# ScalarE's order of work in a hybrid attention block: the probability copy put ahead of the exponentials, eight weight high parts put ahead of a wait

## The chip, the cores and the metric

The kernel runs on one core of a Trainium2 chip, as one program written engine by engine: TensorE (PE) multiplies, ScalarE (ACT) and VectorE (DVE) work elementwise, GpSimd (POOL) does too, SyncE (SP) issues most transfers. The metric is the time of one execution in device microseconds. All times below are microseconds from the start of the profiled execution's span unless they are marked otherwise.

## What is computed

The reference is one layer on an input of 1024 tokens by 1024 features, in float32:

```python
h = rms_norm(x, g_mix[l])
p = h @ w_in[l]
aq, ak, av, mq, mk, mv, mo, mi, mf = jnp.split(p, split_idx, axis=-1)
...
att = sliding_window_attention(aq, ak, av, attn_sinks[l], slopes)
...
mix = jnp.concatenate([rms_norm(att, g_attn_out[l]), rms_norm(mh, g_mlstm_out[l])], axis=-1)
x = x + mix @ w_out[l]
h2 = rms_norm(x, g_ffn[l])
x = x + (jax.nn.silu(h2 @ w_gate[l]) * (h2 @ w_up[l])) @ w_down[l]
```

The attention has 8 query heads and 2 key-value heads of width 64, a window of two chunks of 64 keys, a distance penalty and a learned sink for each head. `mh` is the output of a chunkwise matrix-memory recurrence (mLSTM).

## The kernel before

The tokens are cut into T = 8 tiles of 128. Each large product is computed as three PE passes on split operands, high part times high part and the two cross terms (`three`, lines 878 to 880), so each weight block needs a high part (`w_hi`, a copy with rounding) and a low part (`w_lo`, the remainder). For the key-value weights, eight blocks of 128x264, ScalarE makes the high parts (`w_high(n)`, line 1410) and POOL the low ones (`split`, line 739), each waiting for its high part. The blocks of the later groups are 128x512.

The work between the first product and the feed-forward network is a loop over U from 8 to 55, written out for each engine (line 1106 for PE, 1481 for ACT, 1888 for DVE). U // 8 is the group of columns and U % 8 the tile. Units 8 to 15 make keys, values and gates, 16 to 31 the mLSTM inputs, 32 to 39 the queries, and 40 to 55 are the output projection (`out_unit`, two parts of 12 matmuls). Nothing reorders this: every engine takes its instructions in the written order, and each waits for counted semaphores.

At the start ScalarE sums the squares of the rows of x, computes the row scales (`row_scales`), and sends them through memory to every partition: `store_rows(b)` waits for a transpose by DVE (`rpadT`) and issues four stores, `load_rows(b)` waits for these and issues one load. DVE meanwhile runs the short convolution (lines 1820 and 1822). ScalarE later applies a table change and a SiLU to each convolution result (line 1491).

The attention of tile t takes several values of U. With s = U - 32:

- PE transposes the normalised queries of tile s - 1 (line 1010), ScalarE copies them out as `qT` (line 1544), and PE computes the scores of tile s - 2 (line 1027) after them.
- DVE adds the penalty (line 2086), finds the row maxima `nmx` (lines 2096 and 2097), and ScalarE takes eight exponentials in place in `prob` (line 1582) and one of the sinks (`esk`, line 1585), for tile s - 2.
- In the next U, DVE inverts the sums (lines 1851 and 1852) and normalises one half of `prob` (line 1855); POOL normalises the other half (`normalise`, line 762), and then splits one block of the output weights (lines 735, 737 and 739).
- In the middle of the unit after that, PE transposes the eight blocks of `prob` of tile s - 4 (`att_prob_transposes`, line 1040). ScalarE copies the first half to `pT` (line 1536), DVE the second (line 1846). At the unit's end PE multiplies them with the values (`att_values`, line 1065). This product also waits for `qT` of tile s - 1.
- DVE scales the raw queries to `qn` (line 2107), after the row maxima of the same U. Units 38 and later wait for `qn` because it empties their accumulator bank; the second part of unit 40 waits for `qn` of tile 7.

Of the kernel before, what the change touches and what calls it, by code (L numbers as in the profile page):

```python
# [30 lines left out]
ACT = mybir.ActivationFunctionType  # L31
# [43 lines left out]
def hymba_block(nc, x, g_mix, w_in, b_gates, conv_qk, q_gain, k_gain, sinks,  # L75
# [3 lines left out]
    T = S // P  # L79
    K = D // P  # L80
# [29 lines left out]
    with ctx:  # L110
# [13 lines left out]
        def sem(name):  # L124
            return ctx.enter_context(nc.semaphore(name))
# [116 lines left out]
        qT, prob, pT = [qT0, qT1], [prob0, prob1], [pT0, pT1]  # L242
# [40 lines left out]
        bank = [banks[i // 2][:, i % 2, :] for i in range(8)]  # L283
# [94 lines left out]
        pt_done = sem("p_transposed")  # L378
        pTa = sem("pT_act")
        pTd = sem("pT_dve")  # L380
        pv_done = sem("pv_done")
# [55 lines left out]
        def raw_count(n):  # L437

            return sum(16 * len(slice_source(m)) for m in range(K + n % RAW, n + 1, RAW))
# [870 lines left out]
        def _(act):  # L1310
            steps = [0]

            def step(ins):
                steps[0] += 1
                ins.then_inc(act_step, 1)

            def link(ins):

                step(ins)
                act.wait_ge(act_step, steps[0])  # L1320

            def inverse_root(out_, sumsq, n):

                link(nc.scalar.activation(out_, sumsq, ACT.Ln, bias=eps_t[0:sumsq.shape[0], 0:1], scale=1.0 / n))
                return nc.scalar.activation(out_, out_, ACT.Exp, scale=-0.5)
# [10 lines left out]
            def row_scales(b):  # L1336

                act.wait_ge(x_sq, 4 * b + 4)
                tt = slice(4 * b, 4 * b + 4)
                inverse_root(rstd[:, tt], stat[:, tt], D).then_inc(rstd_ready, 1)  # L1340

            def store_rows(b):

                act.wait_ge(rstd_turned, b + 1)
                if b == 1:
                    act.wait_ge(rstd_s, 16)
                rows = rstd_dram[b:b + 1, :].rearrange("a (t q j) -> q (a t) j", q=4, j=32)
                for q in range(4):
                    act.dma_start(rows[q], rpadT[32 * q:32 * q + 4, b, :]).then_inc(rows_stored, 16)

            def load_rows(b):
                act.wait_ge(rows_stored, 16 * 4 * (b + 1))
                act.dma_start(rstd_b[:, b * H:(b + 1) * H],
                              rstd_dram[b:b + 1, :].to_broadcast([P, H])).then_inc(rstd_s, 16)
# [45 lines left out]
            def w_high(n):  # L1400

                g, k = 1 + n // K, n % K
                width = NKV if g == 1 else N
                if g == 1:
                    act.wait_ge(w1_s, 16 * 2)
                    w = w1_raw[:, k, :]
                else:
                    act.wait_ge(raw_s[n % RAW], raw_count(n))
                    w = w_raw[:, n % RAW, 0:width]
                nc.scalar.activation(w_hi[:, (g * K + k) % RING, 0:width], w, ACT.Copy).then_inc(w_act_hi, 1)  # L1410
# [17 lines left out]
            for t in range(4, T):  # L1428
                square_sum(t)
            row_scales(1)  # L1430
            for n in range(4):
                w_high(n)
            store_rows(1)
            for n in range(4, K):
                w_high(n)
            load_rows(1)
            act.wait_ge(mq_done, 2)
            w_high(K)
# [42 lines left out]
            for U in range(T, ALL):  # L1481
# [33 lines left out]
                s = U - 3 * T  # L1515
# [12 lines left out]
                if 1 <= s < T:  # L1528
                    state_squares(s - 1)
                s = U - 4 * T  # L1530
                if 0 <= s - 4 < T:
                    tt = s - 4
                    act.wait_ge(pt_done, tt + 1)
                    if tt >= 2:
                        act.wait_ge(pv_done, tt - 1)
                    nc.scalar.activation(pT[tt % 2][:, 0:4, :], bank[6][:, :].rearrange("p (k n) -> p k n", k=4),
                                         ACT.Copy).then_inc(pTa, 1)
                if 0 <= s - 1 < T:
                    tt = s - 1

# [9 lines left out]
                if 0 <= s - 1 < T:  # L1550
                    tt = s - 1
# [10 lines left out]
                if 0 <= s - 4 < T:  # L1562
                    tt = s - 4
# [7 lines left out]
                if 0 <= s - 6 < T:  # L1571
                    tt = s - 6
                    act.wait_ge(ssa_ready, tt + 1)
                    inverse_root(rmix[:, tt, :], ss2[:, tt, :], N).then_inc(rmix_ready, 1)
                if 0 <= s - 2 < T:
                    tt = s - 2
                    act.wait_ge(s_max, tt + 1)
                    if tt >= 1:
                        act.wait_ge(p_ready[0], tt)
                        act.wait_ge(p_ready[1], tt)  # L1580
                    for j in range(8):
                        step(nc.scalar.activation(prob[tt % 2][:, j, :], prob[tt % 2][:, j, :], ACT.Exp, bias=nmx[:, j:j + 1],  # L1582
                                                  accum_out=dsum[:, j:j + 1]))
                    act.wait_ge(sink_shift, tt + 1)
                    nc.scalar.activation(esk[:, :], esk[:, :], ACT.Exp).then_inc(p_exp, 1)
                s = U - 6 * T
# [713 lines left out]
```

## Time and profile before

| | us |
|---|---|
| median of 3 runs | 992.14 |
| lowest and highest run | 991.68, 992.31 |
| the profiled execution | 992.37 |
| its span | 990.6 |
| PE, busy | 983.1 |
| DVE, ACT, POOL, busy | 652.9, 422.9, 667.2 |

The span is the stretch in which engines work; the rest of the profiled execution's time lies around it. PE's clock is granted in full throughout. A row of the timeline gives the start, the duration, the engine, the line, the operation, what is written and read, the shape, how many instructions are merged, and in brackets how long the engine stood idle before and what released it. Matmul durations overlap: the next one starts before the one before has ended, so the distance between starts is what one costs.

### The profile page before, as it was taken

How to read it: one execution, taken by the hardware profiler on the slowest of the kernel's cores; microseconds unless marked ns; L12 is line 12 of the kernel's file. 1: busy time of each engine (PE TensorE's matmuls, PEld its weight loads, DVE VectorE, ACT ScalarE, POOL GpSimd, SP SyncE). 2: the span in 40 equal slices, each digit the busy share in tenths (PEclk: the TensorE clock that was granted, in tenths of full speed). 3: DMA queues.
4: the chain of work that ended last, by engine and by line, in shares of the span. 5: the costliest groups of instructions: out<-in, count | busy, mean ns of one | idle time of the engine just before them, and what ended most of it. 6: DMA issues, size and time to landing. Idle time of an engine off the chain costs nothing.

```text
span 990.6 us, 13176 instructions
## 1 busy us (share of the span) xinstructions
PE 983.1 (99%) x4816; PEld 814.8 (82%) x4816; DVE 652.9 (66%) x808; ACT 422.9 (43%) x868; POOL 667.2 (67%) x529
## 2 busy tenths in 40 slices
PE   9999999999999999999999999999999999999998
PEld 7898888878888888888888888888888888888887
DVE  5596345569843696958757485866748577674485
ACT  5542155467622665525243342524334352433440
POOL 0164466626784328978868777877877787887792
PEclk9999999999999999999999999999999999999999
DMA  8634435541321002121121121122112112112213
GB/s 294 211 85 81 110 79 138 138 164 33 108 65 32 22 22 85 54 64 43 43 86 44 43 73 55 43 60 68 43 43 85 43 43 80 48 42 62 78 58 134
DMA packets 103592, 76.87 MB, mean 78 GB/s; under 512 B 30696, under 2 KB 83944, under 8 KB 103528
## 3 DMA queue, kind: packets, MB, share of 16 engines
q1 hardware_dynamic: 102168, 75.00, 25.2%
q10 hardware_dynamic: 1360, 1.02, 0.4%
q8 instruction: 39, 0.64, 0.3%
q14 instruction: 25, 0.20, 0.1%
HBM read 68.15 MB, written 7.36 MB: 76 GB/s over the span
## 4 chain that ended last, share of the span: by engine, by line
PE 90%; DVE 3%; DMA 2%; ACT 1%; SPq 1%; issue 1%; POOL 0%; ACTq 0%; DVEq 0%
PE banks L878 29%; PE banks L880 28%; PE banks L879 28%; DMA x_in<-in_x 1%; PE banks L1065 1%; PE banks L891 1%; PE banks L968 1%; ACT prob L1582 1%; PE banks L1040 1%; PE banks L980 0%; DMA rstd_b<-rstd_rows 0%; PE banks L1027 0%; DMA rstd_rows<-rpadT 0%; PE banks L990 0%; PE banks L953 0%
## 5 line engine op out<-in xcount | busy, mean ns | idle before, releaser
L808 POOL TENSOR_TENSOR wr_lo<-wr_raw,wr_hi 128x512 fp32r<-128x512 f32 x231 | 319.0, 1412 | 27.1 <-ACT wr_hi L1394 21.9
L802 POOL TENSOR_TENSOR wr_raw<-wr_raw,wr_raw 128x512 f32<-128x512 f32 x132 | 193.6, 1471 | 132.3 <-PE banks L880 72.7
L878 PE MATMUL banks<-hf_hi,wr_hi 128*128 128x512 f32 x616 | 240.2, 390 | 0.0
L879 PE MATMUL banks<-hf_lo,wr_hi 128*128 128x512 f32 x616 | 239.8, 389 | 0.0
L880 PE MATMUL banks<-hf_hi,wr_lo 128*128 128x512 f32 x616 | 239.8, 389 | 0.0
L1394 ACT ACTIVATE wr_hi<-wr_raw 128x512 fp32r<-128x512 f32 x231 | 136.6, 625 | 165.0 <-POOL wr_raw L802 106.0
L2246 DVE TENSOR_TENSOR x<-banks,x 128x1024 f32<-128x1024 f32 x138 | 168.8, 1225 | 51.5 <-PE banks L880 35.2
L878 PE MATMUL banks<-w_hi,actT_hi 128*128 128x512 f32 (+1 forms) x384 | 147.1, 383 | 0.9 <-POOL w_lo L739 0.8
L880 PE MATMUL banks<-w_hi,actT_lo 128*128 128x512 f32 (+1 forms) x384 | 143.3, 373 | 0.0
L879 PE MATMUL banks<-w_lo,actT_hi 128*128 128x512 f32 (+1 forms) x384 | 143.0, 372 | 0.0
L878 PEld LDWEIGHTS banks<-hf_hi,wr_hi 128*128 128x128 f32 x616 | 115.7, 188 | 24.4 <-issue 0.4
L880 PEld LDWEIGHTS banks<-hf_hi,wr_lo 128*128 128x128 f32 x616 | 115.7, 188 | 24.0
L879 PEld LDWEIGHTS banks<-hf_lo,wr_hi 128*128 128x128 f32 x616 | 115.7, 188 | 23.8
L878 PE MATMUL banks<-wr_hi,af_hi 128*128 128x512 f32 x308 | 120.0, 390 | 0.2 <-DVE x L2246 0.2
L879 PE MATMUL banks<-wr_lo,af_hi 128*128 128x512 f32 x308 | 119.9, 389 | 0.0
L880 PE MATMUL banks<-wr_hi,af_lo 128*128 128x512 f32 x300 | 116.8, 389 | 0.0
L2140 DVE TENSOR_TENSOR af_raw<-banks,af_raw 128x512 f32<-128x512 f32 x33 | 22.8, 691 | 128.9 <-PE banks L880 128.9
L739 POOL TENSOR_TENSOR w_lo<-w_raw,w_hi 128x512 fp32r<-128x512 f32 (+1 forms) x48 | 62.0, 1298 | 56.0 <-ACT w_hi L1410 53.4
L2164 DVE TENSOR_TENSOR af_lo<-af_raw,af_hi 128x512 fp32r<-128x512 f32 x75 | 88.8, 1226 | 0.3
L878 PEld LDWEIGHTS banks<-w_hi,actT_hi 128*128 128x128 f32 x384 | 72.2, 188 | 14.8 <-issue 1.4
L880 PEld LDWEIGHTS banks<-w_hi,actT_lo 128*128 128x128 f32 x384 | 72.2, 188 | 12.9
L879 PEld LDWEIGHTS banks<-w_lo,actT_hi 128*128 128x128 f32 x384 | 72.3, 188 | 11.4
(206 smaller groups left out, 1201.5 us busy)
## 6 DMA issues: line engine op xcount, KB each, us to landing
wr_raw<-in_w_up SPq DMA_DIRECT2D x46, 256.0 KB, 3.2
wr_raw<-in_w_gate SPq DMA_DIRECT2D x44, 256.0 KB, 3.4
wr_raw<-in_w_down SPq DMA_DIRECT2D x44, 256.0 KB, 3.1
w_raw<-in_w_in SPq DMA_DIRECT2D x32, 256.0 KB, 3.6
x_in<-in_x SPq DMA_DIRECT2D x4, 1024.0 KB, 13.1
w_raw<-in_w_out SPq DMA_DIRECT2D x16, 256.0 KB, 2.7
x<-in_x SPq DMA_DIRECT2D x8, 512.0 KB, 6.1
out<-x SPq DMA_DIRECT2D x16, 256.0 KB, 2.1
```

The lines of the kernel that those rows point to most:

```text
L739: nc.gpsimd.tensor_tensor(w_lo[:, ring, 0:width], w, w_hi[:, ring, 0:width].bitcast(F32), ALU.subtract).then_inc(w_ready, 1)
L802: nc.gpsimd.tensor_tensor(wr_raw[slot(q, f)][:, :], wr_raw[slot(q, a)][:, :], wr_raw[slot(q, b)][:, :], ALU.subtract).then_inc(wsum, 1)
L808: nc.gpsimd.tensor_tensor(wr_lo[s][:, :], wr_raw[s][:, :], wr_hi[s][:, :].bitcast(F32), ALU.subtract).then_inc(wf_lo, 1)
L878: nc.tensor.matmul(ps, x_hi, wh, start=first, stop=False, skip_group_check=more)
L879: nc.tensor.matmul(ps, x_hi, wl, start=False, stop=False, skip_group_check=more)
L880: return nc.tensor.matmul(ps, x_lo, wh, start=False, stop=last, skip_group_check=more)
L891: last = nc.tensor.transpose(bank[2 + b][:, j * P:(j + 1) * P], h2buf[t % 2][:, (4 * b + j) * P:(4 * b + j + 1) * P], ident[:, :])
L968: last = nc.tensor.matmul(bank[6 + i][:, value_region(pair)], scd[:, 2 * pair + i, :], mvx[:, t, 2 * pair + i, :], start=pair == 0, stop=t ...
L1394: nc.scalar.activation(wr_hi[s][:, :], wr_raw[s][:, :], ACT.Copy).then_inc(wf_hi, 1)
L2140: V_.tensor_tensor(dst[:, :], src[:, :], dst[:, :], ALU.add).then_inc(added, 1)
L2164: V_.tensor_tensor(af_lo[b][f][:, :], af_raw[b][f][:, :], af_hi[b][f][:, :].bitcast(F32), ALU.subtract).then_inc(act_lo_s, 1)
L2246: V_.tensor_tensor(xs, banks[first + h][:, :, :], xs, ALU.add).then_inc(down_add, 1)
```

## The change

There are two moves of ScalarE instructions, and no instruction is added or taken away. At the start, `w_high(4)` to `w_high(7)` stand ahead of `store_rows(1)`, where before they stood behind it. In the attention, the copy of the transposed probabilities to `pT` stood at the head of the body for tile s - 4, ahead of the query copy. Now it stands one U earlier, for tile s - 3, directly ahead of the exponentials of tile s - 2.

```diff
             row_scales(1)
-            for n in range(4):
+            for n in range(K):
                 w_high(n)
             store_rows(1)
-            for n in range(4, K):
-                w_high(n)
             load_rows(1)
             act.wait_ge(mq_done, 2)
             w_high(K)
...
                 s = U - 4 * T
-                if 0 <= s - 4 < T:
-                    tt = s - 4
-                    act.wait_ge(pt_done, tt + 1)
-                    if tt >= 2:
-                        act.wait_ge(pv_done, tt - 1)
-                    nc.scalar.activation(pT[tt % 2][:, 0:4, :], bank[6][:, :].rearrange("p (k n) -> p k n", k=4),
-                                         ACT.Copy).then_inc(pTa, 1)
                 if 0 <= s - 1 < T:
...
                     inverse_root(rmix[:, tt, :], ss2[:, tt, :], N).then_inc(rmix_ready, 1)
+                if 0 <= s - 3 < T:
+                    tt = s - 3
+                    act.wait_ge(pt_done, tt + 1)
+                    if tt >= 2:
+                        act.wait_ge(pv_done, tt - 1)
+                    nc.scalar.activation(pT[tt % 2][:, 0:4, :], bank[6][:, :].rearrange("p (k n) -> p k n", k=4),
+                                         ACT.Copy).then_inc(pTa, 1)
                 if 0 <= s - 2 < T:
                     tt = s - 2
                     act.wait_ge(s_max, tt + 1)
```

ScalarE at the start, before. The rows L1410 with 128x264 are the high parts of the key-value weights, L1349 the stores of the row scales, L1353 their load:

```order
L1324 ACTIVATE rstd<-stat,cols 128x4
L1325 ACTIVATE rstd<-rstd 128x4
L1410 ACTIVATE w_hi<-w_raw 128x264 x4
L1349 DMA rstd_rows<-rpadT 4x32 x4
L1410 ACTIVATE w_hi<-w_raw 128x264 x4
L1353 DMA rstd_b<-rstd_rows 128x512
L1410 ACTIVATE w_hi<-w_raw 128x512
L1447 ACTIVATE kvs<-banks,rstd 128x264
```

The same place after the change, where L1445 is the first evacuation of a key-value unit:

```order
L1324 ACTIVATE rstd<-stat,cols 128x4
L1325 ACTIVATE rstd<-rstd 128x4
L1410 ACTIVATE w_hi<-w_raw 128x264 x8
L1349 DMA rstd_rows<-rpadT 4x32 x4
L1353 DMA rstd_b<-rstd_rows 128x512
L1410 ACTIVATE w_hi<-w_raw 128x512
L1445 ACTIVATE kvs<-banks,rstd 128x264
```

The last four high parts have moved from behind the stores, and their wait, to ahead of them; the load follows the stores directly.

ScalarE in the attention, from the end of U = 36 into U = 38, before. The rows L1582 are the exponentials, L1536 is the copy to `pT`, L1544 that to `qT`:

```order
L1567 ACTIVATE sqb<-banks 128x512
L1568 ACTIVATE actT_hi<-banks 128x4x128
L1582 ACTIVATE prob_137,dsum<-prob_137,nmx 128x128 x8
L1585 ACTIVATE esk<-esk 128x8
L1536 ACTIVATE pT_143<-banks 128x512
L1544 ACTIVATE qT_135<-banks,cols 128x512
L1470 ACTIVATE pq<-banks,rstd 128x512
L1554 ACTIVATE actT_hi<-mh 128x4x128
```

The same place after the change, where L1580 are the exponentials, L1571 is the copy to `pT` and L1535 that to `qT`:

```order
L1558 ACTIVATE sqb<-banks 128x512
L1559 ACTIVATE actT_hi<-banks 128x4x128
L1571 ACTIVATE pT_143<-banks 128x512
L1580 ACTIVATE prob_137,dsum<-prob_137,nmx 128x128 x8
L1583 ACTIVATE esk<-esk 128x8
L1535 ACTIVATE qT_135<-banks,cols 128x512
L1468 ACTIVATE pq<-banks,rstd 128x512
L1545 ACTIVATE actT_hi<-mh 128x4x128
```

The copy to `pT`, with its wait for PE's transposes of that tile, has moved from behind the eight exponentials and `esk` to ahead of them; the copy to `qT` now follows `esk` directly.

## Rows read from the trace of the kernel before

**Rows 1.** Page, first part: busy time of an engine, share, instructions

```profile
PE 983.1 (99%) x4816; PEld 814.8 (82%) x4816; DVE 652.9 (66%) x808; ACT 422.9 (43%) x868; POOL 667.2 (67%) x529
```

**Rows 2.** Waits of PE: us in total, times, longest

```profile
PE banks L1065 <- ACT qT L1544: 1.6, 1, 1.6
...
PE banks L878 <- POOL w_lo L739: 0.8, 2, 0.5
```

**Rows 3.** Timeline of PE, the first key-value unit (U = 8)

```profile
49.76 0.28 PE L878 MATMUL banks<-w_hi,actT_hi 128*128 128x264 f32 x1
...
50.12 0.29 PE L878 MATMUL banks<-w_hi,actT_hi 128*128 128x264 f32 x1
...
54.11 0.28 PE L878 MATMUL banks<-w_hi,actT_hi 128*128 128x264 f32 x1
```

**Rows 4.** Timeline of ACT, then of POOL, 42 to 57 us

```profile
49.12 1.05 ACT L1410 ACTIVATE w_hi<-w_raw 128x264 fp32r<-128x264 f32 x3 [5.71 <-issue]
...
42.55 3.54 POOL L739 TENSOR_TENSOR w_lo<-w_raw,w_hi 128x264 fp32r<-128x264 f32 x4 [40.76 <-ACT w_hi L1410]
49.62 7.36 POOL L739 TENSOR_TENSOR w_lo<-w_raw,w_hi 128x264 fp32r<-128x264 f32 x6 [3.53 <-ACT w_hi L1410]
```

**Rows 5.** Timeline of DVE and PE around the gates (U = 18)

```profile
89.55 0.19 DVE L1918 SCALAR_TENSOR_TENSOR lf<-gate,expf 128x32 f32<-128x32 f32 x1 [4.49 <-ACT expf L1507]
...
90.87 0.30 PE L1114 MATMUL banks<-lf,tri 128*128 128x32 f32 x2
```

**Rows 6.** Timeline of PE in the attention, transposes (L1040) and value products (L1065)

```profile
221.53 0.66 PE L1065 MATMUL banks<-pT,v_prev 128*64 128x128 f32 x8 [1.64 <-ACT qT L1544]
...
225.42 1.03 PE L1040 MATMUL banks<-ident,prob 128*128 128x128 f32 x8
...
230.66 0.66 PE L1065 MATMUL banks<-pT,v_prev 128*64 128x128 f32 x8
...
234.78 1.03 PE L1040 MATMUL banks<-ident,prob 128*128 128x128 f32 x8
```

**Rows 7.** Timeline of ACT in the attention, 217 to 230 us

```profile
217.04 0.40 ACT L1582 ACTIVATE prob<-prob,nmx 128x128 f32<-128x128 f32 x1 [3.17 <-DVE nmx L2097]
...
220.24 0.57 ACT L1536 ACTIVATE pT<-banks 128x512 f32<-128x512 f32 x1
220.71 0.67 ACT L1544 ACTIVATE qT<-banks,cols 128x512 f32<-128x512 f32 x1
...
225.93 0.40 ACT L1582 ACTIVATE prob<-prob,nmx 128x128 f32<-128x128 f32 x1 [1.71 <-DVE nmx L2097]
...
229.68 0.69 ACT L1544 ACTIVATE qT<-banks,cols 128x512 f32<-128x512 f32 x1
```

**Rows 8.** Timeline of DVE, then of POOL, 229 to 236 us

```profile
234.15 0.65 DVE L2097 TENSOR_TENSOR nmx<-nmx,nsink 128x8 f32<-128x8 f32 x1
...
235.66 0.69 DVE L2107 TENSOR_TENSOR qn<-banks,qscale 128x512 f32<-128x512 f32 x1
...
229.74 1.54 POOL L762 TENSOR_TENSOR prob<-prob,dsum 128x512 f32<-128x512 f32 x1 [2.64 <-DVE dsum L1852]
...
233.48 1.29 POOL L739 TENSOR_TENSOR w_lo<-w_raw,w_hi 128x512 fp32r<-128x512 f32 x1
```

**Rows 9.** Timeline of DVE and PE in unit 40: last `qn`, second part

```profile
253.91 0.69 DVE L2107 TENSOR_TENSOR qn<-banks,qscale 128x512 f32<-128x512 f32 x1
...
254.65 0.50 PE L878 MATMUL banks<-w_hi,actT_hi 128*128 128x512 f32 x1
```

**Rows 10.** Timeline of DVE, POOL and PE around unit 42

```profile
273.28 0.68 DVE L1846 COPY pT<-banks 128x512 f32<-128x512 f32 x1
...
270.09 1.29 POOL L739 TENSOR_TENSOR w_lo<-w_raw,w_hi 128x512 fp32r<-128x512 f32 x1
...
263.26 1.03 PE L1040 MATMUL banks<-ident,prob 128*128 128x128 f32 x8
...
275.87 0.66 PE L1065 MATMUL banks<-pT,v_prev 128*64 128x128 f32 x8
```

## The prediction

> **What bounds the kernel now.** I read the busy times first. PE works 983.1 of the 990.6 us of the span [rows 1], so all of its idle time is 7.5 us, and the two moves touch no PE instruction. The second view is the list of PE's waits, which says where ScalarE's order costs PE anything: 1.6 us in one place, a value product waiting for the copy of queries `qT`, and 0.8 us in two places, the first key-value unit waiting for low weight parts [rows 2]. The timelines around these two places give the rest. In both, the thing to see is the distance between starts on PE with nothing late, and how early each of its inputs was. Everything behind them is a long stretch in which PE waits for nothing, so a microsecond won or lost there should reach the end unchanged.
>
> **First edit, the high parts.** Unit 8 on PE takes its triples of matmuls 0.36 us apart while nothing is late (49.76, 50.12), so its eight triples need 2.88 and unit 9 would start at 52.64. It starts at 54.11 [rows 3]. The late inputs are the low parts of blocks 4 to 7: POOL stood idle 3.53 us for their high parts, and ScalarE made these from 49.12 on, after 5.71 us without work behind the wait for the row scales [rows 4]. With the change ScalarE makes them in that idle stretch, from about 43.4, at 0.35 each (1.05 for three), done at 44.8. POOL made the first four low parts in 3.54, 0.885 each, to 46.09, and goes straight on with the other four, to 49.6. Block 4 is wanted at 51.2. PE waits for none of them: **54.11 - 52.64 = 1.47 us gained**.
>
> What hides the moved work is ScalarE's idle stretch of 5.71 us, of which 1.4 are used. The stores, which come behind, were waiting for DVE and leave as before. What the earlier POOL work may cost is DVE's time: it now runs beside the turning of the row scales, before 49.12. If DVE were held for one low part at each of two small instructions, the stores would leave 1.8 later, near 51, and the load and the next high part would follow; unit 8 ends at 52.64 and only then does ScalarE have to evacuate it. So I take nothing, with 0 and 1.8 us on a covered path as the ends.
>
> Does the gain live on? PE's next close meeting is at unit 18, where the gate sums were ready at 89.74 and wanted at 90.87 [rows 5]. They came out of ScalarE (`expf`), which had been started by the evacuation of unit 17, that is by PE. So they move with PE and the slack of 1.1 stays. What does not move with PE is DVE's convolution before it; were it the last input, at most 1.47 - 1.13 = 0.34 would be lost. From there to unit 32 I let the whole stage move by 1.47.
>
> **Second edit, unit 36.** All times in this part are on the clock of the trace before. ScalarE's exponentials of tile 1 start at 217.04 and the next thing, then the `pT` copy, at 220.24, so a set with its sink takes 3.20; the copy delays what follows by 0.47 (220.24 to 220.71); and PE goes on 0.82 after `qT` starts (220.71 to 221.53) [rows 6, 7]. The transposes of tile 0 lie 5.24 ahead of the natural place of the value product (225.42 to 230.66), so near 214.7, done before 216. The `pT` copy therefore runs in an idle moment before 217.04 (3.17 idle there), and `qT` starts at 220.24: **0.47 us gained**, the value product at 221.06. It is not the whole 1.6, because the exponentials themselves are late.
>
> **Second edit, units 37 to 39.** Here the moved wait bites. Call P the moment when the eight transposes of a tile are done (start plus 1.03). Before, the exponentials of tile 2 started at 225.93, while P of tile 1 was 225.42 + 1.03 = 226.45 [rows 6, 7]. Now the exponentials stand behind the copy, which stands behind P. With 0.04 for a signal (DVE's row ended at 234.80 when POOL's ended at 234.77 [rows 8]), they start at P + 0.04 + 0.47 = P + 0.51, and `qT` after them lets PE go on at P + 0.51 + 3.20 + 0.82 = P + 4.53. PE arrives there by itself at P + 4.21 (230.66 - 226.45). So PE loses 0.32 us in each unit. That the margin is this thin shows already in the trace: `qT` started at 229.68, would have let PE go at 230.50, and PE came at 230.66 [rows 6, 7].
>
> Is P really the later of the two inputs in every unit? The maxima are held by POOL. From exponentials to POOL's normalisation it is 3.81 (225.93 to 229.74), and from there to the end of its low part 5.03 (234.77), when the row maxima end too [rows 8]. So maxima are ready 8.9 us after the last exponentials started. PE's period is 9.36 (225.42 to 234.78) plus the new 0.32, so P wins in each: **3 x 0.32 = 0.96 us lost** (units 37, 38, 39). The sum of the edit is now -0.47 + 0.96 = +0.49.
>
> **Second edit, unit 40.** The second part of this unit waits for the last `qn`, which ended at 254.60, and PE went on at 254.65 [rows 9]. `qn` starts 0.89 after the end of POOL's low part (234.77 to 235.66) [rows 8]. On the new clock P of tile 3 is 226.45 + 2 x 9.36 = 245.17 plus the shift at that time, -0.47 + 2 x 0.32 = 0.17, so 245.34. The exponentials of tile 4 start at 245.85, POOL at 249.66, its low part ends at 254.69, `qn` starts at 255.58 and ends at 256.27, and PE goes on at 256.32. That is 1.67 after 254.65, so the shift jumps **from 0.49 to 1.67**.
>
> **Second edit, unit 42.** P of tile 5 is 263.26 + 1.03 + 1.67 = 265.96, the exponentials of tile 6 start at 266.47, POOL ends its low part 8.84 later at 275.31. DVE's own `pT` copy started 1.90 after that point (273.28 against 270.09 + 1.29) and takes 0.68, so it ends at 277.89, and PE wants it at 275.87 + 1.67 = 277.54 [rows 10]. With 0.05 for the signal PE loses 0.4, and the edit stands at **+2.1**. Behind it the exponentials are over and nothing else hangs on ScalarE's order.
>
> **Sum.** -1.47 + 2.1 = +0.6 us. The profiled execution has 992.37, so it would have 993.0; the median of the runs is 0.23 below it, at 992.14, which gives **992.8 us**. A measurement of this kernel tells about 0.2% (2 us) from no change.
>
> **A rule beside a row.** The row maxima on DVE (line 2097, a tiny instruction) took 0.65 us and ended within 0.03 of POOL's low part [rows 8]. The Trainium skill, page "SBUF — State Buffer", section "Who interferes with whom", says that a DVE instruction with two inputs in SBUF is blocked while a GpSimd instruction that reads SBUF runs; by that rule, the trace agrees. It speaks against the first edit, since POOL's four low parts come to lie over DVE's work of 46 to 49.6 us; the third rival is what it would make of the time.
>
> **Rivals.**
> - The stalls of the attention are smaller than worked out. Each of the 0.32 rests on sums of starts; if PE arrives later or the copy costs less, only the jumps go. With no stall at units 37 to 42, the result is -1.47 - 0.47 = -1.9 us, 990.2. For it: PE's margin was positive before. Against it: exponentials behind P is plain order, and `qn` hangs on the same chain. Chance 0.07.
> - The stalls at 37 to 39 come and those behind them don't, since DVE is freer than I think: -1.47 + 0.49 = -1.0, 991.2. Chance 0.15.
> - Slower: the gain at the start is lost before unit 32, because DVE, held by POOL from 46 us on, ends the convolutions later and the gates with them, and the attention's loss stays. It gives 992.14 + 2.1 = 994.2, the edge of what can be told; it decides if DVE is over 1.1 us later at unit 18. If in addition the stall of 0.32 repeats in units 40 and 41, it is 994.9. For it: DVE was busy without a break there. Against: the contention is moved rather than added. Chance 0.13.
> - The copy's move does nothing at all, because PE's transposes are early: only the start counts, 990.7. P at 226.45 against 225.93 speaks against it. Chance 0.03.
>
> **Numbers.** My forecast has 0.62. Its cases and the second rival end within 2 us. Slower by over 0.2% (above 994.1) is most of the third rival: 0.11. Faster by over 0.2% (below 990.2) is half of the first and some unseen gain: 0.06. The rest, 0.83, is no change. The range goes from 991.0, which takes in the second rival, to 994.3, which takes in the third's first form.
>
> **What would show it.** In the profile after: unit 9 starts on PE near 52.6; POOL's eight small low parts follow each other; the wait of PE for low parts is gone. In the attention each set of exponentials starts directly behind a `pT` copy, half a microsecond after PE's transposes, and PE's wait for `qT` is spread over four units, about 1.2 in the first and 0.3 in the others. PE waits some 1.5 us in unit 40 for `qn` and some 0.4 in unit 42 for DVE's `pT`. I am wrong if units 37 to 39 keep 9.36 between transposes, or if the units before 32 are not about 1.5 us earlier.

## The result and the profile after

| | median | lowest to highest | profiled execution | its span |
|---|---|---|---|---|
| before | 992.12 us | 991.32 to 993.19 (16 runs) | 992.37 us | 990.6 us |
| after | 993.78 us | 993.12 to 995.01 (16 runs) | 993.57 us | 991.8 us |

The ratio is 1.0019, with a 95% interval from 1.0012 to 1.0026: the change costs 1.66 us in the medians and 1.2 us between the two profiled executions. The forecast was a cost of 0.6 us. The time lies in the range and counts as no change by the forecast's bound of 0.2%, but its interval is wholly on the slow side and reaches past that bound, so the result is a small loss rather than nothing.

The first part of the page, to stand against [rows 1], and the list of PE's waits, to stand against [rows 2] (us in total, times, longest), both of the kernel after:

```profile
PE 983.3 (99%) x4816; PEld 814.7 (82%) x4816; DVE 657.4 (66%) x808; ACT 422.5 (43%) x868; POOL 667.3 (67%) x529
...
PE banks L1065 <- ACT qT L1535: 1.9, 3, 1.2
PE banks L878 <- DVE qn L2105: 1.2, 1, 1.2
...
PE banks L1065 <- issue: 0.4, 1, 0.4
```

PE does the same work in the same time. The wait for low parts is gone, and the one wait for `qT` has become three. Two waits are new: one for `qn`, and one of a value product in unit 42, which the list puts down to no releaser ("issue"). DVE's copy to `pT` is the last input there, ended at 277.00 with the product at 277.11 (DVE, after):

```profile
276.33 0.67 DVE L1844 COPY pT<-banks 128x512 f32<-128x512 f32 x1
```

The kinds of waits are those that the prediction said would be seen. One of its signs of being wrong did come: it asked for the units before 32 to be about 1.5 us earlier, and they are 1.0 earlier, as follows.

The start, PE's timeline after (start, length, engine, line, operation), against [rows 3] and [rows 5]:

```profile
50.52 0.28 PE L878 MATMUL banks<-w_hi,actT_hi 128*128 128x264 f32 x1
...
53.40 0.28 PE L878 MATMUL banks<-w_hi,actT_hi 128*128 128x264 f32 x1
...
89.88 0.30 PE L1114 MATMUL banks<-lf,tri 128*128 128x32 f32 x2
```

Unit 8 takes exactly the 2.88 us worked out, with no wait. It starts at 50.52 and not at 49.76, so unit 9 starts only 0.71 earlier than before (53.40 against 54.11), and the gates of unit 18 are 0.99 earlier (89.88 against 90.87). At the first query transposes, where the attention begins, the lead is 1.03 (195.85 against 196.88).

The attention, PE's timeline after, to stand against [rows 6, 9, 10]:

```profile
195.85 0.60 PE L1010 MATMUL banks<-ident,qn 128*128 128x128 f32 x4
...
220.00 0.66 PE L1065 MATMUL banks<-pT,v_prev 128*64 128x128 f32 x8 [1.16 <-ACT qT L1535]
...
223.89 1.03 PE L1040 MATMUL banks<-ident,prob 128*128 128x128 f32 x8
...
229.56 0.66 PE L1065 MATMUL banks<-pT,v_prev 128*64 128x128 f32 x8
...
239.33 0.66 PE L1065 MATMUL banks<-pT,v_prev 128*64 128x128 f32 x8 [0.37 <-ACT qT L1535]
...
253.21 1.03 PE L1040 MATMUL banks<-ident,prob 128*128 128x128 f32 x8
...
255.45 0.50 PE L878 MATMUL banks<-w_hi,actT_hi 128*128 128x512 f32 x1 [1.21 <-DVE qn L2105]
...
277.11 0.66 PE L1065 MATMUL banks<-pT,v_prev 128*64 128x128 f32 x8 [0.37 <-issue]
...
291.78 0.28 PE L1000 MATMUL banks<-ones,sqb 128*128 128x1 f32 x2
```

Read it as a distance from the first row, since everything before it only moves the clock. From 195.85 to the last product of squares, at the end of unit 44, it is 95.93 us. Before it was 93.65, from the first to the last of these rows of PE (before; the one between is the transposes of unit 40):

```profile
196.88 0.63 PE L1010 MATMUL banks<-ident,qn 128*128 128x128 f32 x4
...
253.50 1.03 PE L1040 MATMUL banks<-ident,prob 128*128 128x128 f32 x8
...
290.53 0.28 PE L1000 MATMUL banks<-ones,sqb 128*128 128x1 f32 x2
```

**The second edit costs 2.28 us** in this pair of executions, in four steps: PE gains 0.50 in unit 36, and loses 0.41 in each of units 37 to 39, 1.09 in unit 40 and 0.44 in unit 42. The stall in unit 37 has no bracket in its row, but shows in the distances: the value product comes 5.67 after its transposes (229.56 - 223.89), where it was 5.24. The transposes from 223.89 to 253.21 are three periods of 9.77; before they were 9.36.

Why ScalarE is late stands in its own timeline after, against [rows 7]:

```profile
224.96 0.60 ACT L1571 ACTIVATE pT<-banks 128x512 f32<-128x512 f32 x1 [2.25 <-PE banks L1040]
225.45 0.39 ACT L1580 ACTIVATE prob<-prob,nmx 128x128 f32<-128x128 f32 x1
...
228.63 0.67 ACT L1535 ACTIVATE qT<-banks,cols 128x512 f32<-128x512 f32 x1
```

The copy waits 2.25 us for the transposes, which end at 223.89 + 1.03 = 224.92. The eight exponentials follow it directly, 0.53 us after that end (P + 0.53 in the prediction's terms), and `qT` after them. The row maxima of this tile were there at 224.86 (next block), before the copy was done: the exponentials start 0.59 us after them, behind the copy. DVE, then POOL, after, against [rows 8]:

```profile
223.64 1.22 DVE L2095 TENSOR_TENSOR nmx<-nmx,nsink 128x8 f32<-128x8 f32 x1
...
223.55 1.28 POOL L739 TENSOR_TENSOR w_lo<-w_raw,w_hi 128x512 fp32r<-128x512 f32 x1
```

The tiny minimum with the sink ends with POOL's low part again, within 0.03 us, and now lasts 1.22 for a work that took 0.65 before. It starts sooner relative to POOL, so the hold shows longer.

### The profile page after: what moved, and what is told of

Same layout as the page of the kernel before. It is cut to its first block, busy times and chain, and to the rows that moved or that the text cites. A ratio compares the mean times of both kernels' runs of the same rounds, so it can differ in the third digit from the quotient of the medians.

```text
span 991.8 us, 13176 instructions
## 1 busy us (share of the span) xinstructions
PE 983.3 (99%) x4816; PEld 814.7 (82%) x4816; DVE 657.4 (66%) x808; ACT 422.5 (43%) x868; POOL 667.3 (67%) x529
## 4 chain that ended last, share of the span: by engine, by line
PE 94%; DVE 3%; ACT 2%; issue 1%; DMA 0%; SPq 0%; ACTq 0%; DVEq 0%
PE banks L878 28%; PE banks L880 28%; PE banks L879 28%; PE banks L933 2%; PE banks L937 1%; PE banks L942 1%; ACT prob L1580 1%; PE banks L1065 1%; PE banks L891 1%; PE banks L968 1%; PE banks L1040 1%; PE banks L980 0%; PE banks L990 0%; PE banks L953 0%; DVE prob L2084 0%
## 5 line engine op out<-in xcount | busy, mean ns | idle before, releaser
L2244 DVE TENSOR_TENSOR x<-banks,x 128x1024 f32<-128x1024 f32 x138 | 168.8, 1224 | 51.5 <-PE banks L880 35.2
```

The source lines that it names most:

```text
L2244: V_.tensor_tensor(xs, banks[first + h][:, :, :], xs, ALU.add).then_inc(down_add, 1)
```

## The experiments

Two theories stood against each other on the start: the edit gives back PE's whole wait in unit 8 (1.47), or part of it is lost again or was never there. On the attention: the copy's wait ahead of the exponentials makes the stalls, or late row maxima do. All the kernels of this section ran on one chip, in two groups of runs, each group with its own runs of the kernel before (992.24 us in the first, 992.12 in the second). A stage distance below is always that of PE from the first query transposes to the last product of squares, as above.

**The kernel before again**, run like a changed one, to see how far two executions of one program differ.

> The kernel before, unchanged, for its profile on the same chip: both theories expect the same time as before and, at the start, a scatter of unit 8's first matmul that does not come from the edits; theory A expects it to be as large as the 0.8 us by which unit 8 started later in the profile of the change.

Measured: 992.13 us (991.82 to 992.44), ratio 1.0000 [0.9992, 1.0009]. Its stage distance is 93.62 us, against 93.65: one program repeats this distance within 0.03 us here, from two executions. Its start is not so steady. PE's timeline, unit 8's first matmul, a wait inside unit 8, and unit 9:

```profile
50.53 0.28 PE L878 MATMUL banks<-w_hi,actT_hi 128*128 128x264 f32 x1
...
53.39 0.39 PE L878 MATMUL banks<-w_hi,actT_hi 128*128 128x264 f32 x1 [0.18 <-POOL w_lo L739]
...
53.87 0.28 PE L878 MATMUL banks<-w_hi,actT_hi 128*128 128x264 f32 x1
```

The same program starts unit 8 at 50.53 where the trace of before has 49.76 [rows 3], and yet reaches unit 9 at 53.87 and not at 54.11. Here the wait for low parts is worth some 0.5 us, not 1.47.

**The first edit alone.**

```diff
-            for n in range(4):
+            for n in range(K):
                 w_high(n)
             store_rows(1)
-            for n in range(4, K):
-                w_high(n)
             load_rows(1)
```

> Only the first edit: all eight high parts ahead of the wait for the row scales. Theory A (the start edit gains, the attention edit loses): unit 9 starts 2.88 us after unit 8 where it was 4.35 before, the whole later stage is 1.5 us earlier, and the median is 1.2 to 1.5 us below before (ratio 0.9985 to 0.9988). Rival B (the start edit gives nothing, because something else in the first 90 us takes its place): the median is within 0.4 us of before, and unit 18 is reached at the same time as before.

Measured: 991.25 us (990.43 to 992.37), ratio 0.9992 [0.9983, 1.0001]: 1.0 us below before, with an interval that just takes in no change. Its stage distance is 93.60, unchanged, as it must be. In the profiled execution unit 8 starts late, at 51.01, because PE had waited for the weights of the very first product:

```profile
9.71 1.17 PE L933 MATMUL banks<-actT_hi,w_hi 128*128 128x512 f32 x4 [1.06 <-ACT w_hi L1398]
...
51.01 0.28 PE L878 MATMUL banks<-w_hi,actT_hi 128*128 128x264 f32 x1
...
53.89 0.28 PE L878 MATMUL banks<-w_hi,actT_hi 128*128 128x264 f32 x1
```

Unit 9 is then reached at 53.89, no sooner than in the kernel before run again (53.87). So the edit does what it says, with unit 8 at 2.88 us, and is worth as much as the start of unit 8 allows.

**The second edit alone.**

```diff
-                if 0 <= s - 4 < T:
-                    tt = s - 4
...
-                    nc.scalar.activation(pT[tt % 2][:, 0:4, :], bank[6][:, :].rearrange("p (k n) -> p k n", k=4),
-                                         ACT.Copy).then_inc(pTa, 1)
...
+                if 0 <= s - 3 < T:
+                    tt = s - 3
...
+                    nc.scalar.activation(pT[tt % 2][:, 0:4, :], bank[6][:, :].rearrange("p (k n) -> p k n", k=4),
+                                         ACT.Copy).then_inc(pTa, 1)
                 if 0 <= s - 2 < T:
                     tt = s - 2
```

> Only the second edit: every copy of transposed probabilities ahead of the next exponentials. Theory A: the median is 2.1 to 2.5 us above before (ratio 1.0021 to 1.0025), made of -0.5 in unit 36, +0.4 in each of units 37 to 39, +1.1 in unit 40 and +0.4 in unit 42. Rival B: it makes the whole loss of the change by itself, 1.2 to 1.7 us, and the start edit adds nothing.

Measured: 994.30 us (994.01 to 994.70), ratio 1.0023 [1.0014, 1.0031]: 2.06 us above before. Its stage distance is 96.27 us, which is 2.6 above the 93.65. That is 0.3 more than in the kernel after. 0.16 of it is the stall of tile 2 (0.53 where that has 0.37). Most of the rest lies in unit 36, which gains 0.37 and not 0.50: the value product comes 24.28 us after the first query transposes, against 24.65 before and 24.15 after, since the maxima and with them the exponentials are 0.12 us later in this distance. It has the same waits as the kernel after; PE's list:

```profile
PE banks L1065 <- ACT qT L1537: 2.1, 3, 1.2
PE banks L878 <- DVE qn L2107: 1.2, 1, 1.2
...
PE banks L1065 <- issue: 0.4, 1, 0.4
```

The loss is the copy's own and needs nothing of the first edit.

**The copy moved for tiles 0 to 2 only**, the others left in their old place: if each moved copy costs by itself, the loss ends where the moved copies end.

```diff
-                if 0 <= s - 4 < T:
+                if 0 <= s - 4 < T and s - 4 >= 3:
...
+                if 0 <= s - 3 < T and s - 3 < 3:
```

> The second edit for tiles 0 to 2 only; the copies of tiles 3 to 7 stay behind the exponentials; no start edit. Theory A (exponentials wait behind the copy; the last scaled queries and DVE's copy hang on the same chain): the exponentials of tile 4 start with the row maxima again, 0.8 us earlier than with all copies moved, so the wait in unit 40 shrinks from 1.2 to about 0.8 and the one in unit 42 is gone: 0.9 us above before (0.6 to 1.3). Rival C (the waits in units 40 and 42 come from something else than the late copies): still 1.8 or more above before.

Measured: 993.18 us (992.62 to 993.72), ratio 1.0010 [1.0001, 1.0019]: 0.94 above before. The stage distance is 94.61, 0.96 above before, so time and distance agree. PE's timeline, value products of tiles 2 and 3, and unit 40:

```profile
240.52 0.66 PE L1065 MATMUL banks<-pT,v_prev 128*64 128x128 f32 x8 [0.37 <-ACT qT L1544]
...
249.91 0.66 PE L1065 MATMUL banks<-pT,v_prev 128*64 128x128 f32 x8
...
255.78 0.50 PE L878 MATMUL banks<-w_hi,actT_hi 128*128 128x512 f32 x1 [0.75 <-DVE qn L2114]
```

The stall is there for the last moved copy and gone for the first that was not moved. The wait for `qn` in unit 40 is shorter by 0.46, about the one stall that is missing, and the wait in unit 42 is gone, as was expected. This is the picture of the copy ahead of the exponentials, once per moved copy, and a `qn` that carries the delay on. It speaks against a cause that would act on all tiles alike.

**First edit, and the copy of tile 0 alone moved.** It asks how much of the gain of unit 36 stays.

```diff
-                if 0 <= s - 4 < T:
+                if 0 <= s - 4 < T and s - 4 >= 1:
...
+                if 0 <= s - 3 < T and s - 3 < 1:
```

> The first edit, and the second for tile 0 only. Theory A: unit 36 gains 0.5 us, but unit 37 then waits for the query copy, whose margin was 0.16, so it gives 0.3 back: together 1.6 us below before, 0.15 below the first edit alone. Rival D (what unit 36 gains stays): 1.9 to 2.0 us below before, 0.5 below the first edit alone.

Measured: 990.99 us (990.23 to 992.26), ratio 0.9989 [0.9980, 0.9998]: 1.25 below before, where 1.6 was expected, and 0.26 below the first edit alone, which is within the noise. The stage distance is 93.65, that of the kernel before: the gain of 0.50 in unit 36 was given back whole. PE's timeline:

```profile
224.41 1.03 PE L1040 MATMUL banks<-ident,prob 128*128 128x128 f32 x8
...
230.01 0.66 PE L1065 MATMUL banks<-pT,v_prev 128*64 128x128 f32 x8
```

The value product of unit 37 comes 5.60 after its transposes, not 5.24. With PE 0.5 us earlier and the exponentials where they were, the next `qT` is the late one by 0.36, of which 0.3 was expected; most of the rest goes in a wait of 0.2 for `qn` in unit 40, which was not. The step that I had left out is that a gain on PE shortens the slack of every later input too, if that did not move with it.

This kernel also shows the third rival in small. Its row scales for the convolution came late, and ScalarE's SiLU with it; ACT, then PE:

```profile
69.57 1.06 ACT L1489 ACTIVATE qkT<-qkT 128x1024 f32<-128x1024 f32 x1 [2.23 <-DVE qkT L1827]
70.54 0.46 ACT L1445 ACTIVATE kvs<-banks,rstd 128x264 f32<-128x264 f32 x1
...
71.05 0.39 PE L878 MATMUL banks<-w_hi,actT_hi 128*128 128x264 f32 x1 [0.29 <-ACT kvs L1445]
```

An evacuation of PE's banks stood behind a SiLU that waited for DVE, and PE waited 0.29 for it. From unit 9 to unit 18 this execution takes 37.09 us; the kernel after and the first edit alone take 36.48. Most of DVE's delay was there before the moved high parts ran: its scaling of the rows ahead of the convolution began at 42.43, against 41.02 in the kernel after, and the first high part started at 43.54. So the moved work did not start it; what did was not tried by itself.

**First edit, and the sink as a column of the scores.** The maxima are what unit 36 waits for. Here each block of scores gets a column that holds the sink, and one reduction over 129 columns takes the place of a reduction and a minimum; the other uses of `prob` read the first 128 columns, so the kernel computes the same.

```diff
-        prob0, e = place("prob0", [P, 8, P], at=e)
+        prob0, e = place("prob0", [P, 8, P + 1], at=e)
...
+                        if kv == 0 and tt < 2:
+                            V_.tensor_copy(prob[tt][:, :, P], sink_b[:, :])
...
-                    link(V_.tensor_reduce(nmx[:, :], prob[tt % 2][:, :, :], AX.X, ALU.max, negate=True))
-                    V_.tensor_tensor(nmx[:, :], nmx[:, :], nsink[:, :], ALU.min).then_inc(s_max, 1)
+                    V_.tensor_reduce(nmx[:, :], prob[tt % 2][:, :, :], AX.X, ALU.max,
+                                     negate=True).then_inc(s_max, 1)
```

> The first edit, copies where they stood before, and the row maxima without their second instruction: the sinks stand as a 129th column of each block of prob, so that one reduction gives the maximum over scores and sink and no tiny DVE instruction waits for the end of POOL's low part. Theory E (POOL holds that tiny instruction, and through it the exponentials, so the maxima are 0.2 to 1.3 us late in each tile): exponentials of tile 1 start 1.2 us earlier, PE's wait in unit 36 falls from 1.6 to 0.4, no wait comes up in unit 37, the 0.36 in unit 40 goes too: 1.3 to 1.7 us below the first edit alone, 2.3 to 2.7 below before. Rival F (the next small instructions are held in its place and the time of the exponentials does not change): the same as the first edit alone, 1.0 below before.

Measured: 989.40 us (988.80 to 991.12), ratio 0.9977 [0.9968, 0.9986]: 2.7 below before, the first kernel here whose gain is large beside the noise. The stage distance is 92.10, 1.50 shorter than with the first edit alone, and this is what the column gives by itself: 1.13 of it in unit 36 (the transposes of tile 4 lie 55.45 after the first query transposes and not 56.58), 0.37 in unit 40. DVE, POOL and ACT of this kernel:

```profile
212.80 1.23 DVE L2097 TENSOR_REDUCE nmx<-prob 128x8 f32<-128x1032 f32 x1
214.06 1.00 DVE L2100 TENSOR_TENSOR esk<-sink_b,nmx 128x8 f32<-128x8 f32 x1
...
213.74 1.29 POOL L739 TENSOR_TENSOR w_lo<-w_raw,w_hi 128x512 fp32r<-128x512 f32 x1
...
214.06 0.40 ACT L1580 ACTIVATE prob<-prob,nmx 128x128 f32<-128x128 f32 x1 [2.13 <-DVE nmx L2097]
```

The reduction runs through while POOL is at work and ends at 214.03, a microsecond before POOL (215.03), and the exponentials start at once. The instruction that is now held to POOL's end is `esk` (214.06 + 1.00 = 215.06), for which nobody waits here. The Trainium skill, page "SBUF — State Buffer", section "Who interferes with whom", says that an instruction of DVE with two SBUF inputs contends with a GpSimd instruction that reads SBUF, and that `tensor_reduce` on trn2 never does. The trace agrees with both: 1.23 us for the reduction under POOL, and an end within 0.03 of POOL's for `esk`.

**The same, with the copy of tile 0 moved**, by the condition of the kernel with the first edit and that copy.

> As e5, with the copy of tile 0 ahead of the exponentials of tile 1. Theory E: the rest of the wait in unit 36 goes as well: 0.3 to 0.4 below e5, 2.7 to 3.1 below before. Rival F: as the first edit with copy 0 alone, 1.2 below before.

Measured: 989.56 us (988.79 to 990.99), ratio 0.9977 [0.9968, 0.9986]: equal to the kernel just above, where 0.3 to 0.4 less was expected. The stage distance is 91.91, 0.19 shorter, so there is a gain, but a small one, and the scatter of the start is larger than it. PE's wait for `qT` fell from 0.55 to 0.26, and a third to a half of that went in the next unit, as in the kernel without the column.

**Both edits and the sink column**: the kernel after with the diff above. If late maxima made the stalls of units 37 to 39, this kernel loses them. If the copy's wait makes them, they stay.

> Both edits as in the change, and the sink column of e5. With all copies ahead of the exponentials these wait for PE's transposes, not for the maxima. Theory A with E: units 37 to 39 still lose 0.3 to 0.4 each, since earlier maxima don't help, and the chain behind the late exponentials stays: 1.5 to 2.5 us above e6, and 0.5 to 1.5 below before. Rival F (the exponentials were late because of the maxima, not because of the copy's wait): the three stalls go and it equals e6.

Measured: 993.06 us (991.54 to 993.50), ratio 1.0005 [0.9996, 1.0014]. It was expected below before, and is 0.9 above. Against the kernel just above it was expected 1.5 to 2.5 us slower: the medians differ by 3.5, the stage distances by 2.45 (94.36 against 91.91). DVE, ACT and PE:

```profile
222.38 1.23 DVE L2097 TENSOR_REDUCE nmx<-prob 128x8 f32<-128x1032 f32 x1
...
224.95 0.60 ACT L1571 ACTIVATE pT<-banks 128x512 f32<-128x512 f32 x1 [2.26 <-PE banks L1040]
225.45 0.39 ACT L1580 ACTIVATE prob<-prob,nmx 128x128 f32<-128x128 f32 x1
...
239.36 0.66 PE L1065 MATMUL banks<-pT,v_prev 128*64 128x128 f32 x8 [0.36 <-ACT qT L1535]
...
255.32 0.50 PE L878 MATMUL banks<-w_hi,actT_hi 128*128 128x512 f32 x1 [1.08 <-DVE qn L2108]
```

The maxima are there at 223.61, 1.84 us before the exponentials start, and the stalls stay: the transposes of tiles 1 to 4 are 9.80, 9.76 and 9.76 us apart, where the kernel with the column and no copy moved has 9.36 to 9.39. **So the copy's wait, and not the maxima, makes the stalls of units 37 to 39**: this is the run that decides it. In unit 42 it is otherwise. There PE no longer waits in this kernel (transposes of tile 5 to value product of tile 6: 12.63 us, against 12.61 before and 13.05 after), so that loss needed the second instruction of the maxima on DVE as well as the moved copy. The miss in the total fits a late start: unit 8 began at 51.52 in the profiled execution, unit 9 at 54.40, so the first edit gave nothing at all in it. That the median of the eleven runs has the same cause is not shown.

## Why the prediction was right, and where it was off

**The first edit: the mechanism was right, the size was one execution's.** "Its eight triples need 2.88" held in every kernel with the edit (50.52 to 53.40, 51.01 to 53.89). "So unit 9 would start at 52.64" did not: it takes the start of unit 8 at 49.76 as given. It is not. The ten profiled executions have 49.76, 50.53, 49.74 and 51.72 without the first edit, and 50.52, 51.01, 50.44, 49.77, 50.44 and 51.52 with it (two of them, 50.44, of different kernels), so the scatter is there without the edit too, and even between two executions of one program (49.76, 50.53). Without the edit, POOL's low parts hide a late unit 8: unit 9 starts at 54.11, 53.87, 53.81 and 54.60. With it, the same lateness reaches unit 9, at 53.40, 53.89, 53.32, 52.66, 53.32 and 54.40. The gain is 1.15 to 1.45 where unit 8 is at 49.77 (52.66 against 53.81 and 54.11), about 0.5 where it is at 50.5 (53.40 against 53.87), and nothing at 51.7. The mis-sized term is thus the 1.47, which measured 1.0 in the medians of the first edit alone. The spread of the runs points the same way: 0.6, 0.7 and 1.1 us from lowest to highest in the three kernels without the edit that had eleven runs each, 1.9 to 2.3 in those with it. It is not proof: the kernel before spread over 1.3 and 1.4 us in its 32 and 33 runs there, and over 1.9 in its 16 runs beside the kernel after. The kernel with first edit and sink column shows it best, with eight runs from 988.80 to 989.78 and three from 990.86 to 991.12.

**The cover of the moved work held.** I had taken nothing for it, with 1.8 us on a covered path as the other end. ACT after:

```profile
42.22 2.61 ACT L1410 ACTIVATE w_hi<-w_raw 128x264 fp32r<-128x264 f32 x8
48.89 1.29 ACTq L1349 DMA_DIRECT2D rstd_rows<-rpadT  x4
```

The stores leave at 48.89, 1.1 us later than before, and not "as before": DVE's small copy for them lasted 0.72 us beside POOL's low parts, against 0.16 before, and began 0.55 later, 0.38 of it from the three convolution instructions ahead of it (3.47 us, against 3.09). PE waited for none of it, as forecast.

**Unit 36** was sized at -0.47 and measured -0.50. **Units 37 to 39** were sized at 0.32 each and measured 0.41. The order of events was right, and the two spans in it were each a little longer: the exponentials start at P + 0.53, not P + 0.51, and from them to PE's going on it is 4.11 us (225.45 to 229.56), where I had added 3.20 and 0.82. So PE goes on at P + 4.64 instead of P + 4.53, against its own P + 4.21. **Unit 40**: the jump was put at +1.18 and is +1.09. The level that it reaches is 1.83 and not 1.67, because of the stalls ahead of it. I had not seen that the kernel before already waited here: its second part began 1.15 after its transposes [rows 9], and only 0.79 when `qn` is early, as with the sink column. **Unit 42**: put at +0.4, measured 0.44. The sum of the edit, 2.1 forecast, is 2.28 in the profile and 2.06 in the run of the second edit alone.

**The sum.** The rise was forecast at 0.6 us and measured 1.66 in the medians: direction and mechanism were right, the size was not, and the time is in the range because the range was wide (991.0 to 994.3). In the profiled execution I forecast 993.0 and it is 993.57. Of the 0.57 that is missing, 0.44 is the start (a lead of 1.03 and not 1.47 at the first query transposes) and 0.2 the attention. The medians of the two edits alone, -1.0 and +2.06, add up to 1.07; the change measured 1.66. The 0.6 between them is within what the intervals allow (each is 0.9 us to either side) and I don't explain it further. Sixteen runs after fall in two groups again, nine from 993.12 to 993.79 and seven from 994.35 to 995.01, and their median is the upper edge of the first.

**The rivals.** Smaller stalls, or none behind unit 39: refuted, by the kernel after and by the second edit alone. The copy does nothing: refuted, since it costs 2.06. The start gain lost through a late DVE: not in the kernel after, whose stretch from unit 9 to 18 is as short as any (36.48); 0.6 us were lost in that way in one other kernel, whose DVE was late for the most part before the moved work began. So the time came nearer to this rival's 994.2 than to the forecast's 992.8, but by another way: the start's own scatter and larger stalls.

## What to carry to other kernels

An instruction moved ahead of others on an engine brings its wait along, and everything behind it then starts after that wait: compare when its input arrives with when theirs do, in the steady loop and not only in the one unit where the gain is seen. A wait read from one execution is an offer only as large as the arrival at it is steady; run the unchanged kernel once more and see whether the place moves before putting its whole length in a sum. And when the late input is a tiny two-input VectorE instruction beside GpSimd, take the instruction away rather than reorder its users: this gave 1.5 us here in the stage distance (2.7 in the medians together with the first edit), where moving the copies cost 2.1 to 2.3.

## What the runs showed of the hardware

The first product's matmuls run at half pace in some executions. The first group of four matmuls after, in the kernel with the copies of tiles 0 to 2 (where the second group is slow too), and in the first edit with the sink column:

```profile
5.62 2.01 PE L933 MATMUL banks<-actT_hi,w_hi 128*128 128x512 f32 x4 [0.22 <-ACT w_hi L1398]
```

```profile
5.64 2.04 PE L933 MATMUL banks<-actT_hi,w_hi 128*128 128x512 f32 x4 [0.24 <-ACT w_hi L1398]
7.49 1.91 PE L937 MATMUL banks<-actT_lo,w_hi 128*128 128x512 f32 x4
```

```profile
5.74 1.16 PE L933 MATMUL banks<-actT_hi,w_hi 128*128 128x512 f32 x4 [0.63 <-ACT w_hi L1398]
```

The group takes 1.15 to 1.17 us in four executions and 1.84 to 2.05 in five, and each slow group puts unit 8 some 0.7 to 1.1 later: about 49.76 with none, 50.4 to 50.5 with one, 51.5 and 51.7 with two. The two executions that don't fit this had no group so slow (1.15 and 1.44) but late weights, a wait of 1.06 us for `w_hi` with the first edit alone (its row is above) and one of 0.59 with the copy of tile 0 moved:

```profile
17.31 1.16 PE L933 MATMUL banks<-actT_hi,w_hi 128*128 128x512 f32 x4 [0.59 <-ACT w_hi L1398]
```

The rows of the granted clock do not tell the slow stretch from the others (the first stretch of the kernel with the copies of tiles 0 to 2, which is slow, and then of the first edit with the sink column, which is not; columns: window, length, PE busy with its matmuls, granted clock, DMA share, GB/s):

```profile
5.50:7.40 1.90, 1.76 (x4) 1.00 0.98 308
```

```profile
5.50:7.40 1.90, 1.66 (x7) 1.00 0.90 264
```

Both give 1.00, which is 2.4 GHz, though four matmuls fill the one stretch and seven the other. The pace of the slow groups is about half, which is also the ratio of the clock's two levels (1.2 and 2.4 GHz), so a lower clock that these rows do not show is one possible cause; no run here tests it. What sets the pace, and why it differs between executions of one program, stays open.

The other thing was a small copy of 128 x 4 elements on DVE, with one input: 0.16 us beside an idle POOL, 0.72 beside POOL's low parts, and 0.71 or 0.72 in the five other profiled kernels with the first edit. The rule that the prediction leaned on is for instructions with two inputs. The Trainium skill, page "SBUF — State Buffer", section "Who interferes with whom", also lists `copy` among the operations that can take the shared ports when their operands meet certain conditions. Whether this copy meets them is not shown here; its 0.72 us beside POOL agrees with it.
